# Streaming encoder step: the samples' product with the values in two steps, and a short attention with all streams in each step

## What is computed

```python
# A: sliding window of 128 frames, 8 query heads on 2 key heads, with a learned sink in the softmax
scores = einsum('btkgd,bskd->bkgts', qg, k) * SCALE            # k: 128 cached + 16 new frames
p = _softmax_with_sink(scores, sink);  out = einsum('bkgts,bskd->btkgd', p, v)
# B: differential, 4 heads of 2 halves each
p = softmax(where(mask, scores, NEG_INF));  attn = p[:, :, 0] - lam * p[:, :, 1]
out = einsum('bhts,bshd->bthd', attn, v)                       # samples: 2048 cached + 16 new frames
# C: forgetting attention, 16 heads, with a running log forget value on both sides
scores = scores + cq[..., :, None] - ck[..., None, :]
out = einsum('bhts,bshd->bthd', softmax(where(mask, scores, NEG_INF)), v)
```

## Time and profile before

| | us |
|---|---|
| median of 3 runs (lowest, highest) | 3747.98 (3741.02, 3748.75) |
| the profiled execution's own time | 3731.06 |
| its span, from the first to the last instruction | 3729.0 |
| TensorE (matmul) busy | 3421.6 (92%) |
| VectorE, ScalarE, GpSimd busy | 1602.2, 1118.7, 254.3 |
| short sample attention, from 377.2 to 430.5 | 53.3 |
| differential attention, prompt and samples, from 431.5 to about 751 | 320 |
| forgetting attention, prompt and samples, from 2102.4 to about 2735 | 633 |

### The profile page before, as it was taken

The page is one execution under the profiler, slowest core; times in us unless marked ns, Lnnn a source line. Parts: engine busy times, 40 slices in busy tenths (PEclk is TensorE's granted clock), DMA queues, the critical chain, the costliest instruction groups (busy, mean ns, idle before and its releaser), DMA issues. The chain is left out here.

```text
span 3729.0 us, 62974 instructions
## 1 busy us (share of the span) xinstructions
PE 3421.6 (92%) x25000; PEld 2921.0 (78%) x25000; DVE 1602.2 (43%) x2934; ACT 1118.7 (30%) x2312; POOL 254.3 (7%) x340
## 2 busy tenths in 40 slices
PE   8998499978999999997999799989978999999997
PEld 7877367667999999996889656665657999999996
DVE  5418366554333333326231266656534333323334
ACT  4215245443111121113222245544433111112211
POOL 2310000023000000004000000000013000000003
PEclk9999699989999999998999899999989999999999
DMA  5438499543111111112553599989553111111102
GB/s 172 122 127 171 117 334 301 193 162 119 45 34 45 45 45 34 38 41 91 156 178 119 170 315 300 310 274 306 184 183 129 55 45 34 40 50 45 34 24 106
DMA packets 399665, 493.22 MB, mean 132 GB/s; under 512 B 69745, under 2 KB 251537, under 8 KB 399313
## 3 DMA queue, kind: packets, MB, share of 16 engines
q1 hardware_dynamic: 399456, 490.36, 42.3%
HBM read 407.10 MB, written 84.10 MB: 132 GB/s over the span
## 5 line engine op out<-in xcount | busy, mean ns | idle before, releaser
L2528 DVE TENSOR_TENSOR f_gated<-f_gated,f_up 128x384 f32<-128x384 f32 x132 | 73.1, 554 | 734.3 <-ACT f_gated L2458 734.3
L2552 DVE TENSOR_TENSOR f_y<-f_y,f_down 128x512 f32<-128x512 f32 x396 | 269.7, 687 | 229.4 <-PE f_down L2647 229.3
L2634 PE MATMUL f_gate<-m_ht_hi,f_w_hi 128*128 128x384 f32 x1056 | 354.8, 336 | 12.1 <-DVE f_w_lo L2579 12.1
L2634 PE MATMUL f_gate<-m_ht_hi,f_w_lo 128*128 128x384 f32 x1056 | 354.5, 336 | 0.0
L2634 PE MATMUL f_gate<-m_ht_lo,f_w_hi 128*128 128x384 f32 x1056 | 354.4, 336 | 0.0
L2634 PE MATMUL f_up<-m_ht_hi,f_w_lo 128*128 128x384 f32 x1056 | 352.7, 334 | 0.0
L2634 PE MATMUL f_up<-m_ht_hi,f_w_hi 128*128 128x384 f32 x1056 | 352.7, 334 | 0.0
L2634 PE MATMUL f_up<-m_ht_lo,f_w_hi 128*128 128x384 f32 x1056 | 352.7, 334 | 0.0
L2647 PE MATMUL f_down<-f_wo_hi,f_act_hi 128*128 128x512 f32 x792 | 313.4, 396 | 10.6 <-DVE f_y L2552 9.3
L2647 PE MATMUL f_down<-f_wo_hi,f_act_lo 128*128 128x512 f32 x792 | 309.8, 391 | 0.0
L2647 PE MATMUL f_down<-f_wo_lo,f_act_hi 128*128 128x512 f32 x792 | 309.6, 391 | 0.0
(11 more groups left out here) (391 smaller groups left out, 6759.0 us busy)
## 6 DMA issues: line engine op xcount, KB each, us to landing
jc_kc<-in_cache_c_k SPq DMA_DIRECT2D x64, 1024.0 KB, 10.5
jc_vc<-in_cache_c_v SPq DMA_DIRECT2D x64, 1024.0 KB, 9.3
jb_kc<-in_cache_b_k SPq DMA_DIRECT2D x32, 1024.0 KB, 11.7
jb_vc<-in_cache_b_v SPq DMA_DIRECT2D x32, 1024.0 KB, 10.5
m_raw<-in_w_ffn_in SPq DMA_DIRECT2D x44, 512.0 KB
f_raw<-in_w_ffn_in SPq DMA_DIRECT2D x44, 512.0 KB
f_raw_o<-in_w_ffn_out SPq DMA_DIRECT2D x22, 1024.0 KB, 6.4
m_raw<-x SPq DMA_DIRECT2D x18, 512.0 KB, 4.1
```

The lines of the kernel that those rows point to most:

```text
L2528: dve.tensor_tensor(prod[:, b], silu[:, b], up[:, q, 0:gw], ALU.mult).then_inc(prod_done, 1)
L2552: dve.tensor_tensor(part, part, down[:, half, :], ALU.add).then_inc(added, 1)
L2634: last = pe.matmul(acc[:, q, 0:gw], a[:, s, k, u, :], b[:, k, token], start=(k == 0 and j == 0), stop=(k == KT - 1 and j == 2))
```

## The change

In `joint_attention` the groups of probabilities are now in the order of the keys, with the new frames last, and lie in banks 0, 1, 0, 0, 0. The exponential is made in two halves, of 1024 columns at step 2 and 1040 at step 3; two sums are added by VectorE, at step 4 and not 3. Groups 0 and 1 are turned at step 3, ahead of the prompt product, the first half of the product (8 tiles) and group 2 at the end of step 4, group 3 at step 5, and group 4 with the second half of the product behind the prompt product of step 5. ScalarE copies the first half of the scores at the head of step 7, no longer at its end, and groups 0 and 1 at step 3.

In `sample_window` all eight streams go through each step together: keys in three banks (`trios`), turned probabilities in groups of four streams (`fours`); copies, maxima and sums work on a group at once. The keys have a semaphore of their own, and the values are loaded last.

```diff
@@ joint_attention @@
-    PG = [(tiles - 1, tiles)] + [(a, a + 4) for a in range(0, tiles - 1, 4)]
+    PG = [(a, min(a + 4, tiles)) for a in range(0, tiles, 4)]
+    bank_of = (0, 1, 0, 0, 0)
-    probs_at = ((), (), (), (), (0, 1, 2), (3, 4), (), ())
+    probs_at = ((), (), (), (0, 1), (), (3,), (), ())
...
             def turn_probs(u, gi):
+                a, b = PG[gi]
+                pe.wait_ge(s_exp_done, 2 * u + (1 if b <= per * 2 else 2))
+                pe.wait_ge(s_copied, 4 * (u + 1))
+                if gi >= 2:
+                    pe.wait_ge(pt_copied, len(PG) * u + (1, 3, 4)[gi - 2])
+                for t in range(a, b):
+                    m = P if t < tiles - 1 else FRAMES
+                    c = (t - a) * P
+                    last = pe.transpose(s_ps[0:m, bank_of[gi], c:c + P], s_probs[:, t * P:t * P + m], ident[:])
+                last.then_inc(pt_done, 1)
+
+            def attend_sample(u, part):
+                pe.wait_ge(pt_copied, len(PG) * u + (2, 4)[part])
...
+                for t in ((range(0, 2 * per), range(2 * per, tiles))[part]):
...
                     if 1 <= u <= U and s == 5:
-                        attend_sample(u - 1)
+                        turn_probs(u - 1, 4)
+                        attend_sample(u - 1, 1)
...
                     if n % 2 == 0:
                         turn_back((n - 2) // 2)
+                    if 1 <= u <= U and s == 4:
+                        attend_sample(u - 1, 0)
+                        turn_probs(u - 1, 2)
...
@@ ScalarE @@
+                part = slice(0, PAST // 2) if half == 0 else slice(PAST // 2, keys)
+                act.activation(s_probs[:, part], s_scores[:, part], ACT.Exp, bias=s_neg[:, 3:4],
+                               accum_out=s_total[:, half:half + 1]).then_inc(s_exp_done, 1)
...
+                    if u < U and s == 7:
+                        copy_scores(u, 0)
                     exponential(n + 2)
                     if n % 2 == 0:
                         copy_output((n - 2) // 2)
+                    if u >= 1 and s == 3:
+                        exponential_sample(u - 1, 1)
                     copy_prompt(act, n + 1)
...
-                        exponential_sample(u - 1)
+                        exponential_sample(u - 1, 0)
...
+                    if u >= 1 and s == 4:
+                        copy_probs(act, u - 1, 2)
+                    if u >= 1 and s == 5:
+                        copy_probs(act, u - 1, 4)
...
-                    if u < U and s == 7:
-                        copy_scores(u, 0)
...
@@ VectorE @@
             def inverse_sample(u):
-                dve.wait_ge(s_exp_done, u + 1)
-                dve.reciprocal(s_inv[:, u % 2:u % 2 + 1], s_total[:]).then_inc(s_inv_done, 1)
+                dve.wait_ge(s_exp_done, 2 * (u + 1))
+                dve.tensor_tensor(s_total[:, 0:1], s_total[:, 0:1], s_total[:, 1:2], ALU.add).then_inc(s_total_done, 1)
...
@@ sample_window @@
+    trios = [(0, 3), (3, 6), (6, STREAMS)]
+    fours = [(0, 4), (4, STREAMS)]
...
+            pe.wait_ge(k_loaded, 32)
+            for a, b in trios:
+                for x in range(a, b):
+                    turned = keys_of(k_ps, x)
+                    pe.transpose(turned[:, 0:P], kc[:, x], ident[:])
+                    last = pe.transpose(turned[:, P:keys], kn[:, x], ident[0:FRAMES, 0:FRAMES])
+                last.then_inc(k_turned, 1)
+            pe.wait_ge(q_done, A_KV)
+            for g, (a, b) in enumerate(trios):
+                pe.wait_ge(kt_done, g + 1)
+                for x in range(a, b):
+                    last = pe.matmul(keys_of(s_ps, x), q_blocks[:, x], kt[:, x], start=True, stop=True)
+                last.then_inc(s_done, 1)
+            for h, (a, b) in enumerate(fours):
+                pe.wait_ge(norm_done, b)
...
+                    pe.transpose(p_ps[:, h, c:c + P], probs[:, x, 0:WIN], ident[:])
+                    last = pe.transpose(pn_ps[0:FRAMES, h, c:c + P], probs[:, x, WIN:keys], ident[:])
+                last.then_inc(p_turned, 1)
+            pe.wait_ge(v_loaded, 32)
+            for h, (a, b) in enumerate(fours):
+                pe.wait_ge(pt_done, 2 * (h + 1))
+                pe.wait_ge(exp_done, STREAMS)
+                for x in range(a, b):
+                    c = (x - a) * P
+                    pe.matmul(o_ps[:, h, c:c + P], vc[:, x], probs_t[:, x], start=True, stop=False)
+                    last = pe.matmul(o_ps[:, h, c:c + P], vn[:, x], probs_tn[:, x], start=False, stop=True)
+                last.then_inc(pv_done, 1)
```

More of the change, by code:

```diff
@@ L1586, in turn_probs @@
+                last.then_inc(pt_done, 1)
+            def attend_sample(u, part):
+                pe.wait_ge(pt_copied, len(PG) * u + (2, 4)[part])
+                if part == 0:
                     pe.wait_ge(s_copied, 4 * (u + 1))
                 else:
[L1588 to L1592 removed]
@@ new lines, in attend_sample @@
+                for t in ((range(0, 2 * per), range(2 * per, tiles))[part]):
+                    new = t == tiles - 1
+                    m = FRAMES if new else P
+                    if new:
+                        pe.wait_ge(pt_copied, len(PG) * (u + 1))
+                    elif t % per == 0:
+                        pe.wait_ge(vc_loaded[t // per], 16 * (u + 1))
+                    for j in range(4):
+                        values = vn[:, j * P:(j + 1) * P] if new else vc[:, t // per, t % per, j * P:(j + 1) * P]
+                        last = pe.matmul(o_ps[32 * j:32 * j + 32, :], s_probs_t[0:m, t, 32 * j:32 * j + 32], values,
+                                         start=(t == 0), stop=new, skip_group_check=True)
@@ L1613, in turn_output @@
+                if part == 1:
+                    last.then_inc(s_pv_done, 1)
             def turn_output(u):
```

211 lines of the change are left out of this document (84 added, 127 removed).

## The result

The changed kernel takes **3694.3 us** (median of 3 runs, 3686.8 to 3696.7) against 3748.0 (3741.0 to 3748.8) before: ratio 0.986, 95% interval 0.983 to 0.989, some 54 us less. The profiled execution took 3686.8 (span 3685.0), 44.2 less than the one of before (3731.1, span 3729.0).

| stage | before, from | long | after, from | long | difference |
|---|---|---|---|---|---|
| all ahead of it | 0 | 377.2 | 0 | 378.3 | +1.1 |
| short sample attention (sa) | 377.19 | 54.3 | 378.29 | 35.5 | -18.9 |
| differential attention (jb) | 431.50 | 322.0 | 413.74 | 318.4 | -3.5 |
| merge, forward, projections | 753.45 | 1348.9 | 732.15 | 1351.9 | +3.0 |
| forgetting attention (jc) | 2102.35 | 635.3 | 2084.06 | 607.6 | -27.6 |

What follows compares the result with a forecast made beforehand. TensorE's order of work was taken to bound the joint attentions, an engine-to-engine chain the short one. 24 + 16.0 + 6.9 + 1 - 2.4 = 45.5 us off 3747.98 gives 3702.5, range 3680 to 3727.

Steps and rivals of the forecast that it cites:

- Start of the short stage: Short sample attention: with values loaded last, keys alone release the first turn, 3.2 us earlier, at 381.6; between 0 and 4.
- idle time in the middle: Short sample attention, between scores and turns of the probabilities: TensorE idle for 3 us, from 2 to 5.
- Clock of the short stage: Short sample attention: clock rises halfway through the unbroken keys' turns and scores; 24 us won in the stage, bounds 10 and 28.
- Rival (c): Short sample attention: clock stays low because its pieces are too broken; 13 us won instead of 24, 3713; chance 0.12.
- Rival (d): Short sample attention: turns don't raise the clock, scores and late products do; 4 us less won, 3706; chance 0.11.
- Halves, 1.07 a unit: Forgetting attention: exponential in halves turns waits of 1.88 into 0.8; 1.07 us a unit, 15 units, 16.0 us.
- Copy first, 0.49: Forgetting attention: score copies at the head of step 7 remove the 0.49 us wait; 14 units, 6.9 us.
- Differential attention, 1: Differential attention: waits of 0.95 become 0.8 us a unit; 7 x 0.15, 1 us won.
- Last units, 1.2 each given back: Last unit of each joint attention: three groups share one bank; 1.2 us later, from 0.3 sooner to 2 later; 2.4 back.
- Left at zero: Forgetting attention: unowned waits and clock falls priced at nothing; up to 10 + 12 us won, or as much lost.
- Rival (b): Forgetting attention: the unowned waits and clock falls go too, with the smoother stream; 3680; chance 0.17.
- Rival (e): Joint attentions: 0.8 us idle before eight turns brings the clock down in the units, 6.9 us each; 3785; chance 0.04.

Runs made afterwards that it cites:

- the two fillings: Changed kernel with the short sample attention's gap filled by ten useless products or 24 useless turns: 3689.1 us (ratio 0.985) and 3694.8 us (0.987).

## Why the prediction was right, and where not

The forecast was 3702.5 with 45.5 us of gain against the profiled execution; it was 44.0 by spans, 3694.3 by the median. The 8 us between the two medians come from the distance to the profiled execution, which I let stand at 16.9 and which was 7.5. That the gain comes within 1.5 us is luck in good part: the short stage won 5 us less than forecast and the halves some 5, and the unowned stops, left at zero, won 10.

- **Start of the short stage**: taken as 4.4 us behind the first load, measured 5.64. The first turn is now released by the new keys, so the values no longer hold it back, but the keys alone still needed that long; 1.2 us of the term. The idle time in the middle was 2.81 for the 3 taken.
- **Clock of the short stage**: the failed step. I let it rise 5.4 us into the stretch and stay up. It rose after 9 us, fell in the gap (which I had priced at 2 to 3 us: 2.0 and 2.3 by the two fillings) and once more in the products, which I hadn't seen: the earlier trace rows gives TensorE as busy for 29.6 us, and I took that as work, while a good part of the products' time is the spacing between 128 and 16 rows. 24 became 18.9, and 15.9 in the execution where the clock never rose. Rival (c), low clock all through at 13, is what that execution did. Rival (d), 4 us less than the forecast, described the clock better than I did: it rose late in the scores (392.9) and again among the products (399.7). But its reason doesn't hold: turns alone held the clock, and before the change it rose within a stretch of turns.
- **Halves, 1.07 a unit**: the waits of 1.88 went and one of 0.90 came, for the 0.8 worked out. By the unit's length, after the 0.55 of the copy, it is 35.53 - 34.20 - 0.55 = 0.78. Of the waits alone 0.98 should be left; the missing 0.2 I can only argue, from the more and smaller pieces of turns. That the halves are needed is shown: without them 1.7 us a unit are lost.
- **Copy first, 0.49**: 0.55.
- **Differential attention, 1**: the undisturbed units, 34.75 and 34.5 in turn, are now 34.48 and 34.22, so 0.27 less each where 0.15 was forecast; one disturbed unit (38.67 before, with a stop of 2.31) is absent, which is 4 us of luck. Against that the last unit; 3.5 us less in all.
- **Last units, 1.2 each given back**: 2.5 and 3.3, and 1.9 to 3.2 in other profiles of the new order. The mechanism was right (one bank for three groups) and the size was not: I counted 2.9 us of turns and copies, but the low clock, which the broken-up work keeps, doubles products and turns.
- **Left at zero**: the unowned stops and falls. In the forgetting attention they cost 24.6 us before and 14.4 after, 10 us of the measured gain. Rival (b) has come true in part. In this stage stops of 0.3 us and more sum to 11.3 and 14.0 us in the two profiles with the old joint attentions, and to 2.0 to 8.2 in the twelve with the new ones or variants of them. That the order of work softens them fits, as the stream is consumed less fast with the sample's 128 products in two pieces; but this is argued, not shown. The stops are waits for packets of instructions; why one packet comes 2 us late and the next in time isn't settled.
- **Rival (e)**, a fall in each unit, didn't occur at 0.9 us of idleness and did at 1.8, in every second unit: so its mechanism is real, at twice the wait.
- The 3.0 us that the merge and forward stages took longer I did not expect; no line of theirs changed, and over the 14 profiles this stretch takes 1348.9 to 1354.7 us, so it is within what executions differ by.

## What to carry to other kernels

Read a stretch of a busy TensorE by the spacing of its records before counting it as work: products that alternate between 128 and 16 rows took twice their time here, and grouping them (0.27 against 0.42 us) was worth more than the wait that the profile showed. A wait that moves from one line to another is no gain, and its length matters beyond its sum, since 0.9 us left the clock alone and 1.8 did not. And where a change adds or removes instructions, compare undisturbed units, since waits for packets of instructions are tied to the stream, move with it and shift the total by several us. A stop that the list calls "issue" is worth a look at the instruction queue.

## What the runs showed of the hardware that was not expected

- TensorE waited for its instructions: all 89 stops without a releaser, of 0.31 to 3.4 us, in the joint attentions of 14 profiles ended 1.25 to 2.1 us behind a packet of 16384 bytes on the instruction queue. They stand at fixed places of the stream, a multiple of 256 recorded instructions apart and often 1024: 20 records added more than 2100 us earlier moved a stop by 20 records, 24 by 24.
- Products with 128 and 16 rows in turn start 0.42 us apart, with 128 rows only 0.22, grouped by rows 0.27, all at a granted clock of 1.00: each change between 128 and 16 rows costs 0.2 us. In the short stage the clock fell in the midst of unbroken work only among the alternating ones (403.1, 401.8 and 402.0 us in three of the profiles).
- Forty turns in a row, without a product between, kept the granted clock at 1.00.
- Idle pieces of 0.9 us in each unit of 34 us left the clock up; pieces of 1.8 brought it down for 3.4 us in every second unit.
- The same code ran the short stage in 35.3 to 35.7 us in five profiles and in 38.4 to 38.7 in three; the mean granted clock was 0.60 in the changed kernel's first profile and 0.50 in its second.
